# Half of the second feed-forward product by seven block products, their sums made by GpSimd, and four inverse levels with VectorE's transpose

## The chip, the core and the metric

One core of a Trainium2 chip runs the whole kernel. The metric is the device time of one execution in microseconds, the median of the runs shown. Five engines work beside each other, each on its own list of instructions: TensorE (PE; its weight loads are shown apart as PEld), VectorE (DVE), ScalarE (ACT), GpSimd (POOL) and SyncE (SP), which here only issues transfers.

## The reference

All arithmetic is in float32. One decoder block on 256 tokens of width 2048: a gated DeltaNet branch and a sliding-window attention branch, merged by gates, then a feed-forward part with squared ReLU. What the change touches is the last product, and the triangular solve of the DeltaNet branch.

```python
# _gdn_chunked
sol = lax.linalg.triangular_solve(eye + a_kk, rhs, left_side=True, lower=True, unit_diagonal=True)
...
# reference
h = _rmsnorm(x, ln2_w[l])
u = jax.nn.relu(jnp.einsum("bsd,df->bsf", h, w_ff1[l]))      # w_ff1 (2048, 8192)
x = x + jnp.einsum("bsf,fd->bsd", jnp.square(u), w_ff2[l])   # w_ff2 (8192, 2048)
```

## The kernel before, in words

**The stream of weights.** Every weight matrix comes from memory in tiles of four 128-row blocks by 512 columns (1 MB), into four buffers `raw` that are filled in turn. SP issues the transfers in program order; each waits on `lo_ready` until the tile that lies in its buffer is split. A tile is worked in two pieces of [128, 2 blocks, 512]. Float32 precision is kept by splitting each piece in a high and a low part: ScalarE copies the piece to `hi` (line 745, rounded), VectorE takes the difference `lo = raw - hi` (line 1126). Both have four buffers (`PIECES`), so ScalarE and VectorE stay up to four pieces ahead of TensorE: ScalarE waits on `piece_used`, VectorE on `hi_ready`, TensorE on `lo_ready`. Each engine's list is written out by hand: the function `ahead` puts the split of piece m + 4 and whatever step belongs at place m one behind the other, so that a step which waits holds up all splits behind it.

**A product.** `group` (line 387 is its matmul) takes a 512-column output for both token tiles t = 0, 1 into the two banks `acc[:, t]`. One piece against one token tile is six matmuls of 128x128 weights and 512 columns (two blocks, times high-high, low-high and high-low).

**The feed-forward part** runs in two halves of 4096 hidden columns. In each half eight groups (8 pieces each) make `us = relu(...)`, 512 columns at a time; VectorE squares them to `uq` (line 1648); after the first pair of pieces of the next group, TensorE turns `uq` by eight 128x128 transposes (line 403) into the two banks `tb`, from which ScalarE and VectorE write `u_hi` and `u_lo`. Then four groups (`GG0`, `GG1`) of 16 pieces multiply these by `w_ff2`, 512 output columns each, and VectorE adds both banks to `x1`.

**The inverse.** In the stage from about 440 to 665 us the triangular inverse of each head pair is built in `LEVELS` = 6 levels, for four head pairs. A level has `level_a` (line 624, behind GpSimd's masked product `Ls`, line 366) and `level_b`, whose lines 633 and 636 form the correction and its transpose; VectorE subtracts both from the two copies `both_[:, 1]` and `both_[:, 0]`. These steps lie between the matmuls of other groups. GpSimd has nothing to do behind this stage.

## Time and profile before

| what | value |
| --- | --- |
| median of 3 runs | 1557.05 us (1555.12 to 1557.07) |
| the profiled execution, whole | 1553.01 us |
| its span in the trace | 1551.3 us |
| TensorE busy | 1531.9 us, 99% |
| VectorE busy | 927.0 us, 60% |
| ScalarE busy | 741.5 us, 48% |
| GpSimd busy | 55.9 us, 4% |

The span is the part of the profiled execution that the trace covers, from its first to its last instruction or transfer. The profiled execution is one of its own and 4 us below the median, so a sum made on the trace is carried over to the median as a difference. Matmuls overlap their neighbours: a matmul's duration (0.39 us) is longer than the distance from one start to the next, and it is the distance that counts.

### The profile page before, as it was taken

Reading aid. Unit: us, or ns where it says so; the run is one execution under the profiler, and the core shown is the slowest. Engines: PE = TensorE matmul, PEld = TensorE weight load, DVE = VectorE, ACT = ScalarE, POOL = GpSimd, SP = SyncE. Lnnn points to the kernel's source line nnn. Section 1 sums busy time; section 2 is a strip of 40 time slices with the busy share of each in tenths; the row PEclk is TensorE's granted clock in tenths of the full one; section 3 lists DMA queues with packets and bytes.
Section 4 is the critical chain, followed back from the end, with each engine's and each line's share of the span. In section 5 each row is a group of like instructions: output and inputs, shape, how many; then the busy total and the mean of one; then the engine's idle time right before and its main releaser. Section 6 shows DMA issues by size and latency. Waiting matters only on the chain.

```text
span 1551.3 us, 19383 instructions
## 1 busy us (share of the span) xinstructions
PE 1531.9 (99%) x7244; PEld 1277.6 (82%) x7244; DVE 927.0 (60%) x1110; ACT 741.5 (48%) x827; POOL 55.9 (4%) x97
## 2 busy tenths in 40 slices
PE   7999999999999999999999999999999999999999
PEld 5888888888888888878888888888888888888887
DVE  5866645777786876866555555544444555554443
ACT  5554444667654444453445444443333444443332
POOL 5000000000040110100000000000000000000000
PEclk9999999999999999999999999999999999999999
DMA  7565554444544444444655655555556556556552
GB/s 255 190 206 183 189 182 163 156 156 150 164 162 136 147 143 143 136 162 163 244 186 167 198 181 189 189 190 190 189 190 193 186 190 189 187 183 212 204 199 72
DMA packets 140521, 275.96 MB, mean 178 GB/s; under 512 B 7088, under 2 KB 7600, under 8 KB 140208
## 3 DMA queue, kind: packets, MB, share of 16 engines
q1 hardware_dynamic: 136160, 272.71, 52.9%
q10 hardware_dynamic: 4304, 2.47, 0.5%
q8 instruction: 38, 0.62, 0.2%
q14 instruction: 19, 0.16, 0.0%
HBM read 273.06 MB, written 2.10 MB: 177 GB/s over the span
## 4 chain that ended last, share of the span: by engine, by line
PE 96%; DVE 2%; DMA 1%; ACT 1%; ACTq 0%; issue 0%; SPq 0%; DVEq 0%
PE acc L387 88%; PE wk L403 2%; DMA raw<-in_w_in 1%; PE wk L636 1%; PE wk L633 1%; PE wk L624 1%; DVE lo L1126 1%; PE wk L508 1%; PE wk L481 1%; PE wk L468 0%; DVE st_lo L1164 0%; ACT hi L745 0%; PE wk L492 0%; PE wk L519 0%; PE wk L615 0%; PE wk L643 0%
## 5 line engine op out<-in xcount | busy, mean ns | idle before, releaser
L1126 DVE TENSOR_TENSOR lo<-raw,hi 128x1024 fp32r<-128x1024 f32 x512 | 624.8, 1224 | 549.7 <-ACT hi L745 532.0
L745 ACT ACTIVATE hi<-raw 128x1024 fp32r<-128x1024 f32 x512 | 541.9, 1060 | 647.7 <-PE acc L387 645.6
L387 PE MATMUL acc<-hi,st_hi 128*128 128x512 f32 x1312 | 524.5, 400 | 5.6 <-DVE lo L1126 2.9
L387 PE MATMUL acc<-lo,st_hi 128*128 128x512 f32 x1312 | 511.6, 390 | 0.0
L387 PE MATMUL acc<-hi,st_lo 128*128 128x512 f32 x1312 | 511.1, 390 | 0.0
L387 PEld LDWEIGHTS acc<-hi,st_hi 128*128 128x128 f32 x1312 | 246.7, 188 | 55.7 <-DVE lo L1126 4.4
L387 PEld LDWEIGHTS acc<-lo,st_hi 128*128 128x128 f32 x1312 | 246.2, 188 | 52.2
L387 PEld LDWEIGHTS acc<-hi,st_lo 128*128 128x128 f32 x1312 | 246.8, 188 | 47.9 <-issue 1.0
L387 PE MATMUL acc<-hi,u_hi 128*128 128x512 f32 x512 | 199.3, 389 | 0.0
L387 PE MATMUL acc<-lo,u_hi 128*128 128x512 f32 x512 | 199.2, 389 | 0.0
L387 PE MATMUL acc<-hi,u_lo 128*128 128x512 f32 x512 | 199.2, 389 | 0.0
L387 PEld LDWEIGHTS acc<-lo,u_hi 128*128 128x128 f32 x512 | 96.1, 188 | 20.1
L387 PEld LDWEIGHTS acc<-hi,u_hi 128*128 128x128 f32 x512 | 96.1, 188 | 19.9
L387 PEld LDWEIGHTS acc<-hi,u_lo 128*128 128x128 f32 x512 | 96.1, 188 | 19.8
L387 PE MATMUL acc<-hi,mix_hi 128*128 128x512 f32 x128 | 50.2, 392 | 0.0
L387 PE MATMUL acc<-lo,mix_hi 128*128 128x512 f32 x128 | 49.9, 390 | 0.0
L387 PE MATMUL acc<-hi,mix_lo 128*128 128x512 f32 x128 | 49.8, 389 | 0.0
L366 POOL TENSOR_TENSOR Ls<-pair,lmask 128x256 f32<-128x256 f32 x24 | 22.2, 932 | 184.7 <-DVE pair L1468 122.2
L387 PE MATMUL acc<-hi,oa_hi 128*128 128x512 f32 x64 | 25.3, 395 | 3.4 <-DVE oa_lo L1141 3.4
L1141 DVE TENSOR_TENSOR both__109<-both__109,wk 128x256 f32<-128x256 f32 x48 | 19.9, 416 | 14.4 <-PE wk L633 14.2
L387 PEld LDWEIGHTS acc<-lo,mix_hi 128*128 128x128 f32 x128 | 24.0, 188 | 5.0
L387 PEld LDWEIGHTS acc<-hi,mix_lo 128*128 128x128 f32 x128 | 24.0, 188 | 4.9
(246 smaller groups left out, 1048.7 us busy)
## 6 DMA issues: line engine op xcount, KB each, us to landing
raw<-in_w_ff SPq DMA_DIRECT2D x128, 1024.0 KB, 5.1
raw<-in_w_in SPq DMA_DIRECT2D x100, 1024.0 KB, 5.0
raw<-in_w_out SPq DMA_DIRECT2D x16, 1024.0 KB, 5.0
raw<-in_w_gdn_proj SPq DMA_DIRECT2D x8, 1024.0 KB, 5.0
raw<-in_w_swa_proj SPq DMA_DIRECT2D x4, 1024.0 KB, 5.0
x_tok<-in_x SPq DMA_DIRECT2D x2, 1024.0 KB, 7.1
x<-in_x SPq DMA_DIRECT2D x1, 2048.0 KB, 7.9
out_x<-x ACTq DMA_DIRECT2D x3, 512.0 KB, 3.6
```

Source lines behind the costliest of these rows:

```text
L366: pool.tensor_tensor(Ls[:, l % 2], pair[:], bcast(lmask[:, l, :], 1, [P, 2, P]), ALU.mult).then_inc(ev["n_Ls"], 1)
L387: last = pe.matmul(acc[:, t], w[:, k0 + 2 * m + kk, P * t:P * t + P], v[:, i % PIECES, kk, :], start=m == 0 and kk == 0 and a == 0, stop=m ...
L403: last = pe.transpose(dst[:, b, P * t:P * t + P], src(t, b), ident[:])
L481: last = pe.matmul(wk[:, 2 + g * nk // N, g * nk % N:g * nk % N + nk], qc[:, g, P * t:P * t + P], swa_qk[:, 1, HS * g + h, 0:nk], start=Tr ...
L508: last = pe.matmul(wk[:, 4, 0:P], pt[:, P * b:P * b + P], swa_v[:, kt, at:at + P], start=b == 0, stop=b == NG * (t + 1) - 1)
L624: last = pe.matmul(blk(W[0], h), Ls[:, l % 2, h, :], diag[:, 1, h, :], start=True, stop=True)
L633: last = pe.matmul(blk(W[3], h), diag[:, 0, h, :], Pc[:, h, :], start=True, stop=True)
L636: last = pe.matmul(blk(W[2], h), Pc[:, h, :], diag[:, 0, h, :], start=True, stop=True)
L745: act.activation(hi[:, i % PIECES], raw[:, i // 2 % RAW, 2 * (i % 2):2 * (i % 2) + 2, :], ACT.Copy)\
L1126: dve.tensor_tensor(lo[:, i % PIECES], raw[:, i // 2 % RAW, 2 * (i % 2):2 * (i % 2) + 2, :], hi[:, i % PIECES].bitcast(F32), ALU.subtract) ...
L1141: dve.tensor_tensor(out_, a, b, op).then_inc(done, 1)
```

## The change

**The second product** is now made from tiles of `w_ff2` for two neighbouring 512-column groups at a time. The 4096 rows of a half are cut into eight octets of four 128-row blocks. For the even octets the product [2 token tiles x 2 pairs of row blocks] by [2 pairs of row blocks x 2 column groups] is formed by seven block products in place of eight, in the variant of Winograd; the odd octets are multiplied as before. Each of the seven products has one piece of weights and one token tile's weights load: six matmuls. Four of the seven weight pieces (t1, t2, t4, t3) are sums of parts of the octet's two tiles; GpSimd makes them (`weight_sums`, 128x1024 elements each, in four buffers `t_sums`), one behind the other, and they are then split by ScalarE and VectorE like a loaded piece. The matching sums of the squared activations are made by GpSimd too (`token_sums`, 128x256 each), from a copy that ScalarE writes; ScalarE and VectorE split them. The products end in eight banks (p1 to p7, c22), so `acc` and `wk` are both full during this stage. After the last even octet of a column pair VectorE (`first_sums`, `second_sums`) and GpSimd (`shared_sums`) combine the banks into `x1`. A half now has 88 pieces where it had 64, and 720 large matmuls where it had 768. The tiles of an even octet are loaded when the octet two before it has been split and (`octet_used`) its sums are made. The squares are written over `us`, `uq` is gone, and the transposes of the last group come after the second piece of the second product.

**The inverse:** in the levels 0 to 3 the transposed correction (line 636, two matmuls, and the VectorE subtraction of it) is left out, and VectorE transposes `both_[:, 1]` into `both_[:, 0]` instead. This is exact there since everything lies within 32x32 blocks.

```diff
+IN_BLOCKS = 4
+
+OCTETS = 8
+PAIR_PIECES = 11
+HALF_PIECES = 2 * OCTETS // 2 * PAIR_PIECES
+MORE_PIECES = HALF_PIECES - 64
+PRODUCTS = ("b11", "b21", "b22", "t1", "t2", "t4", "t3")
...
+        def pieces_of(half):
+            return [(np_, o, n) for np_ in range(2) for o in range(OCTETS) for n in range(4 if o % 2 else 7)]
...
+        def source(half, np_, o, n):
+
+            t = tile0(half, np_, o)
+            if o % 2 == 0 and n >= 3:
+                return t_sums[n - 3][:], ev["t_made"], sums_before(half, np_, o) + n - 2
+            which, k = (n // 2, 2 * (n % 2)) if o % 2 else ((0, 0), (0, 2), (1, 2))[n]
+            return raw[:, (t + which) % RAW, k:k + 2, :], landed[(t + which) % RAW], 16 * ((t + which) // RAW) + 16
...
+            def octet_used(half, np_, o, which):
+
+                a = piece0(half) + octet0(np_, o)
+                if o % 2:
+                    sp.wait_ge(lo_ready, a + 2 * which + 2)
+                else:
+                    sp.wait_ge(lo_ready, a + 2 + which)
+                    sp.wait_ge(ev["t_made"], sums_before(half, np_, o) + 3 + which)
 
...
+            def token_sums(half, k):
+
+                n = 4 * half + k
...
+                    pool.wait_ge(lo_ready, piece0(0) + octet0(1, 6) + 5)
+                pool.tensor_tensor(s1, a21, a22, ALU.add).then_inc(ev["s_made"], 1)
+                pool.tensor_tensor(s3, a11, a21, ALU.subtract).then_inc(ev["s_made"], 1)
+                pool.wait_ge(ev["s_made"], 4 * n + 1)
+                pool.tensor_tensor(s2, s1, a11, ALU.subtract).then_inc(ev["s_made"], 1)
+                pool.wait_ge(ev["s_made"], 4 * n + 3)
+                pool.tensor_tensor(s4, a12, s2, ALU.subtract).then_inc(ev["s_made"], 1)
...
+            def weight_sums(half, np_, o):
+
+                t = tile0(half, np_, o)
+                made = sums_before(half, np_, o)
+                b11, b21 = raw[:, t % RAW, 0:2, :], raw[:, t % RAW, 2:4, :]
+                b12, b22 = raw[:, (t + 1) % RAW, 0:2, :], raw[:, (t + 1) % RAW, 2:4, :]
+                t1, t2, t4, t3 = (t[:] for t in t_sums)
+
...
+                def free(n):
+                    if np_ or o:
+                        pool.wait_ge(lo_ready, piece0(half) + octet0(*divmod(OCTETS * np_ + o - 2, OCTETS)) + 4 + n)
+                    elif n == 0:
...
+                pool.wait_ge(landed[t % RAW], 16 * (t // RAW) + 16)
+                pool.wait_ge(landed[(t + 1) % RAW], 16 * ((t + 1) // RAW) + 16)
+                free(0)
+                pool.tensor_tensor(t1, b12, b11, ALU.subtract).then_inc(ev["t_made"], 1)
+                free(1)
+                pool.wait_ge(ev["t_made"], made + 1)
+                pool.tensor_tensor(t2, b22, t1, ALU.subtract).then_inc(ev["t_made"], 1)
+                free(2)
+                pool.wait_ge(ev["t_made"], made + 2)
+                pool.tensor_tensor(t4, b21, t2, ALU.subtract).then_inc(ev["t_made"], 1)
+                free(3)
+                pool.tensor_tensor(t3, b22, b12, ALU.subtract).then_inc(ev["t_made"], 1)
+
+            def shared_sums(half, np_):
+                n = 2 * half + np_
+                pool.wait_ge(ev["c_first"], 5 * n + 4)
+                x12, x21, x22 = x1_part(np_, 0, 1), x1_part(np_, 1, 0), x1_part(np_, 1, 1)
+                pool.tensor_tensor(x12, x12, sum2[:], ALU.add).then_inc(ev["c_pooled"], 1)
+                pool.wait_ge(ev["c_first"], 5 * n + 5)
+                pool.tensor_tensor(x21, x21, sum3[:], ALU.add).then_inc(ev["c_pooled"], 1)
+                pool.tensor_tensor(x22, x22, sum3[:], ALU.add).then_inc(ev["c_pooled"], 1)
+
+            for half in range(2):
...
+                        if l < IN_BLOCKS:
+                            return
...
+            def products(half, np_, o, gf):
+
...
+                for m, name in enumerate(PRODUCTS):
+                    if o == 0:
...
+                            pe.wait_ge(ev["c_first"], 5 * n)
+                        if name == "b21":
+                            if np_:
+                                pe.wait_ge(ev["c_second"], 4 * n - 3)
+                            else:
+                                pe.wait_ge(acc_free, 2 * (gf + 8) + 1)
+                        if name == "b22":
+                            if np_:
+                                pe.wait_ge(ev["c_second"], 4 * n - 1)
+                            else:
+                                pe.wait_ge(acc_free, 2 * (gf + 8) + 2)
+                        if name == "t4" and np_ == 0:
+                            pe.wait_ge(ev["u_lo"], 8 * half + 8)
+                    pe.wait_ge(lo_ready, a0 + m + 1)
+                    slot = (a0 + m) % PIECES
+                    wh, wl = factor(u_hi, None, o, combos[name]), factor(u_lo, u_lo6, o, combos[name])
+                    alone = name in ("b11", "t1", "t2", "t3")
+                    for kk in range(2):
+                        for a, (w, v) in enumerate(((wh, hi), (wl, hi), (wh, lo))):
+                            last = pe.matmul(banks[name], w[:, kk, :], v[:, slot, kk, :],
+                                             start=o == 0 and kk == 0 and a == 0,
+                                             stop=alone and o == OCTETS - 2 and kk == 1 and a == 2)
...
+                    pe.wait_ge(ev["u_lo"], 8 * half + o + 1)
+                for j, banks in enumerate(((p2, p4), (p3, c22))):
+                    for t in range(TT):
+                        for m in range(2):
+                            if t == 0:
+                                pe.wait_ge(lo_ready, a0 + 2 * j + m + 1)
+                            begins = o == 1 and j == 1 and t == 1
+                            if begins and m == 0 and n:
+                                pe.wait_ge(ev["c_second"], 4 * n)
+                            slot = (a0 + 2 * j + m) % PIECES
+                            for kk in range(2):
...
+                def parts():
+                    n = 4 * half + g // 2
+                    act.wait_ge(ev["u_turned"], g + 8 * half + 1)
+                    if g:
+                        act.wait_ge(ev["s_made"], 4 * n)
+                    elif half:
+                        act.wait_ge(lo_ready, piece0(0) + octet0(1, 6) + 4)
+                    act.activation(u_copy[:], tbv, ACT.Copy).then_inc(ev["uc_made"], 1)
+                    act.activation(u_hi[g][:, 0:2], tbv[:, :, 0:P].rearrange("p (c k) t -> p c k t", c=2), ACT.Copy)
+                    act.activation(u_hi[g][:, 2], tbv[:, 2:4, P:2 * P], ACT.Copy).then_inc(ev["u_hi"], 1)
+                return plain if g % 2 else parts
...
+            def piece(half, p):
+                src, sem_, value = source(half, *pieces_of(half)[p])
+                act.wait_ge(sem_, value)
+                act.wait_ge(piece_used, piece0(half) + p + 1)
+                act.activation(hi[:, (piece0(half) + p) % PIECES], src, ACT.Copy).then_inc(hi_ready, 1)
...
-                        less(1, ev["n_S2"], ev["n_Ma"])
+                        less(1, (ev["n_S2"], 6 * i + l + 1), ev["n_Ma"])
                         if l < LEVELS - 1:
                             diagonal(1, l + 1, ev["n_Ra"], (ev["n_Ma"], 6 * i + l + 1))
-                        less(0, ev["n_S3"], ev["n_Mb"])
+                        if l < IN_BLOCKS:
+                            dve.wait_ge(ev["n_Ma"], 6 * i + l + 1)
+                            dve.transpose(flat(both_[:, 0]), flat(both_[:, 1])).then_inc(ev["n_Mb"], 1)
+                        else:
+                            less(0, (ev["n_S3"], (LEVELS - IN_BLOCKS) * i + l - IN_BLOCKS + 1), ev["n_Mb"])
...
+            def u_square(g, n):
                 dve.wait_ge(acc_free, 2 * g + 4)
...
+            def piece(half, p):
+                src, _, _ = source(half, *pieces_of(half)[p])
+                a = piece0(half) + p
+                dve.wait_ge(hi_ready, a + 1)
+                dve.tensor_tensor(lo[:, a % PIECES], src, hi[:, a % PIECES].bitcast(F32), ALU.subtract)\
+                    .then_inc(lo_ready, 1)
...
+                def of_p5():
+                    dve.wait_ge(piece_used, a + 4)
+                    dve.tensor_tensor(x12, p5, x12, ALU.add).then_inc(ev["c_first"], 1)
+                    dve.tensor_tensor(x22, p5, x22, ALU.add).then_inc(ev["c_first"], 1)
+
+                def of_p1_p6():
+                    dve.wait_ge(ev["c_copied"], n + 1)
+                    dve.tensor_tensor(x11, p1, x11, ALU.add).then_inc(ev["c_first"], 1)
+                    dve.wait_ge(piece_used, a + 5)
+                    dve.tensor_tensor(sum2[:], p6, sum2[:], ALU.add).then_inc(ev["c_first"], 1)
+
+                def of_p7():
+                    dve.wait_ge(ev["c_first"], 5 * n + 4)
+                    if n:
+                        dve.wait_ge(ev["c_pooled"], 3 * n)
+                    dve.wait_ge(piece_used, a + 7)
+                    dve.tensor_tensor(sum3[:], p7, sum2[:], ALU.add).then_inc(ev["c_first"], 1)
+                return of_p5, of_p1_p6, of_p7
...
+            def second_sums(half, np_):
+
+                n = 2 * half + np_
+                a = piece0(half) + octet0(np_, OCTETS - 1) + PIECES
+
+                def add(t, j, bank, sem_, value, pooled):
+                    def step():
+                        part = x1_part(np_, t, j)
+                        dve.wait_ge(sem_, value)
+                        if pooled:
+                            dve.wait_ge(ev["c_pooled"], 3 * n + pooled)
+                        else:
+                            dve.wait_ge(ev["c_first"], 5 * n + 3)
+                        dve.tensor_tensor(part, bank, part, ALU.add).then_inc(ev["c_second"], 1)
+                    return step
+                return (add(0, 0, p2, ev["c_done"], 2 * n + 1, 0), add(1, 0, p4, piece_used, a + 2, 2),
+                        add(0, 1, p3, ev["c_done"], 2 * n + 2, 1), add(1, 1, c22, piece_used, a + 4, 3))
+
...
+                for np_ in range(2):
+                    at = octet0(np_, OCTETS - 1)
+                    of_p5, of_p1_p6, of_p7 = first_sums(half, np_)
+                    c11, c21, c12, c22_ = second_sums(half, np_)
+                    steps |= {at: of_p5, at + 1: of_p1_p6, at + 2: of_p7, at + 3: c11}
```

Where a column pair of the second product ends and the next begins, VectorE's list was, at the end of one group of 16 pieces (`lo` is a split; x1 the result):

```order
L1126 TENSOR_TENSOR lo_51<-raw_49,hi_50 128x1024 [waits hi_ready] x12
L1626 TENSOR_TENSOR x1_128<-acc,x1_128 128x512 [waits acc0_done,x_back]
L1126 TENSOR_TENSOR lo_51<-raw_49,hi_50 128x1024 [waits hi_ready]
L1630 TENSOR_TENSOR x1_128<-acc,x1_128 128x512 [waits piece_used]
L1126 TENSOR_TENSOR lo_51<-raw_49,hi_50 128x1024 [waits hi_ready]
```

It is now, at the same place (`t_sums0` to `t_sums3` are GpSimd's sums t1, t2, t4, t3 of the next column pair's first octet):

```order
L1922 TENSOR_TENSOR lo_51<-raw_49,hi_50 128x1024 [waits hi_ready]
L1963 TENSOR_TENSOR x1_128<-acc,x1_128 128x512 [waits c_first,c_done]
L1922 TENSOR_TENSOR lo_51<-t_sums0_154,hi_50 128x1024 [waits hi_ready]
L1963 TENSOR_TENSOR x1_128<-wk,x1_128 128x512 [waits c_pooled,piece_used]
L1922 TENSOR_TENSOR lo_51<-t_sums1_155,hi_50 128x1024 [waits hi_ready]
L1963 TENSOR_TENSOR x1_128<-acc,x1_128 128x512 [waits c_pooled,c_done]
L1922 TENSOR_TENSOR lo_51<-t_sums2_156,hi_50 128x1024 [waits hi_ready]
L1963 TENSOR_TENSOR x1_128<-wk,x1_128 128x512 [waits c_pooled,piece_used]
```

The add of `acc` on the sixth row, for which TensorE's third product of the next column pair waits (`c_second`), has moved behind the splits of t1 and t2.

GpSimd's list had nothing at this place; it now has this, from the last even octet of a column pair over the end to the first octet of the next:

```order
L483 TENSOR_TENSOR t_sums_154<-raw 128x1024 [waits lo_ready,landed1,landed0]
L486 TENSOR_TENSOR t_sums_155<-raw,t_sums_154 128x1024 [waits t_made,lo_ready]
L489 TENSOR_TENSOR t_sums_156<-raw,t_sums_155 128x1024 [waits t_made,lo_ready]
L491 TENSOR_TENSOR t_sums_157<-raw 128x1024 [waits lo_ready]
L497 TENSOR_TENSOR x_128<-x_128,sum_131 128x512 [waits c_first]
L499 TENSOR_TENSOR x_128<-x_128,sum_132 128x512 [waits c_first]
L500 TENSOR_TENSOR x_128<-x_128,sum_132 128x512
L483 TENSOR_TENSOR t_sums_154<-raw 128x1024 [waits lo_ready,landed1,landed0]
```

The three adds onto x stand between the four weight sums of one column pair and those of the next.

At the start of the second product TensorE's list had the transposes of the last squares behind 24 matmuls, of which the last three stand here:

```order
L387 MATMUL acc<-hi,u_hi 128x512
L387 MATMUL acc<-hi,u_lo 128x512
L387 MATMUL acc<-lo,u_hi 128x512
L403 MATMUL wk<-ident,uq 128x128 [waits u_lo,u_squared]
L403 MATMUL wk<-ident,uq 128x128 x7
L387 MATMUL acc<-hi,u_hi 128x512 [waits lo_ready]
```

Now they come behind 12 matmuls (the first, and the last three, stand here):

```order
L904 MATMUL wk<-hi,u_hi_133 128x512 [waits lo_ready,s_lo,u_lo]
L904 MATMUL acc<-hi,u_hi_133 128x512
L904 MATMUL acc<-hi,u_lo_141 128x512
L904 MATMUL acc<-lo,u_hi_133 128x512
L546 MATMUL wk<-ident,us 128x128 [waits u_lo,u_squared]
L546 MATMUL wk<-ident,us 128x128 x7
L904 MATMUL acc<-hi,u_hi_133 128x512 [waits lo_ready,acc_free]
```

VectorE's list at that place is now this; the square of `us` for which the transposes wait stands behind the split of `t_sums0`:

```order
L1909 TENSOR_TENSOR u_lo6_s4_151<-u_sums_153,u_hi6_139 128x256
L1922 TENSOR_TENSOR lo_51<-raw_49,hi_50 128x1024 [waits hi_ready]
L1922 TENSOR_TENSOR lo_51<-t_sums0_154,hi_50 128x1024 [waits hi_ready]
L1916 TENSOR_TENSOR us_130<-us_130 128x1024 [waits acc_free]
L1922 TENSOR_TENSOR lo_51<-t_sums1_155,hi_50 128x1024 [waits hi_ready]
L1922 TENSOR_TENSOR lo_51<-t_sums2_156,hi_50 128x1024 [waits hi_ready]
L1391 TENSOR_TENSOR u_lo7_148<-wk,u_hi7_140 128x1024 [waits u_hi]
L1922 TENSOR_TENSOR lo_51<-t_sums3_157,hi_50 128x1024 [waits hi_ready]
```

The square has the place that it had, behind the split of the fourth piece, but that piece and the two behind the square are now sums of GpSimd.

## Rows read from the trace of the kernel before

**Rows 1.** The page: span, busy time by engine, and the chain that ended last.
```profile
span 1551.3 us, 19383 instructions
...
PE 1531.9 (99%) x7244; PEld 1277.6 (82%) x7244; DVE 927.0 (60%) x1110; ACT 741.5 (48%) x827; POOL 55.9 (4%) x97
...
PE 96%; DVE 2%; DMA 1%; ACT 1%; ACTq 0%; issue 0%; SPq 0%; DVEq 0%
```

**Rows 2.** Windows, second product: length, PE, PEld, DVE, ACT, POOL, clock, DMA share, GB/s.
```profile
1017.00:1188.00 171.00, 171.00 (x760) 141.66 (x760) 83.07 (x71) 68.58 (x66) 0.00 (x0) 1.00 0.58 194
```

**Rows 3.** The timeline in the second half's second product: start us, length us.
```profile
1479.70 0.39 PE L387 MATMUL acc<-hi,u_hi 128*128 128x512 f32 x1
...
1481.26 1.06 ACT L745 ACTIVATE hi<-raw 128x1024 fp32r<-128x1024 f32 x1 [3.02 <-PE acc L387]
...
1482.35 2.59 DVE L1126 TENSOR_TENSOR lo<-raw,hi 128x1024 fp32r<-128x1024 f32 x2 [2.85 <-ACT hi L745]
...
1485.60 0.39 PE L387 MATMUL acc<-lo,u_hi 128*128 128x512 f32 x1
```

**Rows 4.** The page's groups of instructions: count, busy us, mean ns, idle before.
```profile
L1126 DVE TENSOR_TENSOR lo<-raw,hi 128x1024 fp32r<-128x1024 f32 x512 | 624.8, 1224 | 549.7 <-ACT hi L745 532.0
L745 ACT ACTIVATE hi<-raw 128x1024 fp32r<-128x1024 f32 x512 | 541.9, 1060 | 647.7 <-PE acc L387 645.6
```

**Rows 5.** The timeline of TensorE at one inverse level.
```profile
457.47 0.60 PE L633 MATMUL wk<-Pc,diag 128*128 128x128 f32 x4
457.91 0.61 PE L636 MATMUL wk<-diag,Pc 128*128 128x128 f32 x4
458.28 0.48 PE L387 MATMUL acc<-hi,st_hi 128*128 128x512 f32 x1
```

**Rows 6.** The timeline of VectorE and GpSimd where both work, first level.
```profile
452.56 0.42 DVE L1141 TENSOR_TENSOR diag<-pair,lbase 128x256 f32<-128x256 f32 x1
452.61 1.86 POOL L366 TENSOR_TENSOR Ls<-pair,lmask 128x256 f32<-128x256 f32 x2 [8.30 <-DVE pair L1468]
...
453.01 0.45 DVE L1473 STREAM_TRANSPOSE both__109<-diag 128x256 f32<-128x256 f32 x1
...
453.38 0.48 DVE L1141 TENSOR_TENSOR both__109<-ident,diag 128x256 f32<-128x256 f32 x1
...
453.79 0.96 DVE L1141 TENSOR_TENSOR both__109<-ident,both__109 128x256 f32<-128x256 f32 x1
```

**Rows 7.** The same, where GpSimd comes behind one of the splits.
```profile
521.43 1.22 DVE L1126 TENSOR_TENSOR lo<-raw,hi 128x1024 fp32r<-128x1024 f32 x1
...
521.85 1.40 POOL L366 TENSOR_TENSOR Ls<-pair,lmask 128x256 f32<-128x256 f32 x1 [4.44 <-PE wk L624]
...
522.57 0.68 DVE L1539 TENSOR_REDUCE small<-o_sq 128x4 f32<-128x512 f32 x1
```

**Rows 8.** GpSimd's instructions by shape: busy us, mean ns.
```profile
L325 POOL MEMSET rmask<- 128x768 f32 x1 | 0.7, 739 | 0.0
...
L326 POOL MEMSET below<- 128x128 f32 x1 | 0.2, 207 | 0.0
```

**Rows 9.** One tile's instructions (Ls): duration ns min/median/max.
```profile
L366 POOL TENSOR_TENSOR Ls<-pair,lmask x24: 727/923/1403, 452.6 to 650.5; 128x256 f32<-128x256 f32 x24
```

**Rows 10.** The timeline where the second product begins, at 1017.3 us.
```profile
1019.16 1.22 DVE L1126 TENSOR_TENSOR lo<-raw,hi 128x1024 fp32r<-128x1024 f32 x1 [0.71 <-ACT hi L745]
...
1020.30 1.22 DVE L1648 TENSOR_TENSOR uq<-us 128x1024 f32<-128x1024 f32 x1
...
1022.74 1.03 PE L403 MATMUL wk<-ident,uq 128*128 128x128 f32 x8
```

**Rows 11.** The page's DMA issues: KB each, us from issue to landing.
```profile
raw<-in_w_ff SPq DMA_DIRECT2D x128, 1024.0 KB, 5.1
```

**Rows 12.** VectorE's adds onto x1 in the same stretch: count, busy us, mean ns.
```profile
L1626 DVE TENSOR_TENSOR x<-acc,x 128x512 f32 (+1 forms) x3 | 2.1, 691 | 1.4 <-PE acc L387 1.4
```

**Rows 13.** The waits: engine, line, what it waited for: us in total, times, longest.
```profile
PE wk L409 <- DMA rows<-in_conv_w: 3.7, 1, 3.7
```

305 lines of the change are left out of this document (216 added, 89 removed).

## The prediction

> **What bounds the kernel now.** I read the page first: TensorE is busy 99% of the span and makes 96% of the chain that ended last [rows 1]. The windows view of one second product shows the same locally: TensorE busy for all of 171 us at granted clock 1.00 (its full level, 2.4 GHz), VectorE 83 us, ScalarE 69 us, GpSimd nothing [rows 2]. The timeline gives the pace: 27 large matmuls start between 1479.70 and 1485.60 us, so one costs 0.227 us and six, the work of one piece against one token tile, 1.36 us. The splits stand idle between pairs: a copy of 1.06 us starts behind the matmuls that free its buffer, the two VectorE splits follow it [rows 3, 4]. So fewer matmuls shorten the kernel as long as the pieces keep coming. That is the question.
>
> **What TensorE saves.** Before, each half of the second product has 768 large matmuls, now 720. 96 fewer by 0.227 are 21.8 us. The transposed correction goes in four levels of four head pairs: 16 times, each from 457.91 to the next large matmul at 458.28, 0.37 us [rows 5]: 5.9 us. Its replacement on VectorE is a transpose of 0.45 us for a subtraction that costs as much as its neighbours of 0.42 [rows 6], with one wait fewer; TensorE does not wait there for VectorE, so this part costs nothing, and if its cover were gone 16 times 0.03 us. Together TensorE has 27.7 us less to do.
>
> **What GpSimd has to do.** Sixteen times (2 halves, 2 column pairs, 4 even octets) it makes four sums of 128x1024. No row has that shape. The shortest product of 128x256 took 0.73 us [rows 9]. Without a fixed part the new sum costs four times that, 2.9 us: the upper bound. The two memsets give a fixed part of 0.10 us (0.207 for 128 elements, 0.739 for 768) [rows 8], which makes 2.6 us. Below, GpSimd took 0.73 us where VectorE takes 0.42 [rows 6, 9], and 1.7 times VectorE's 1.22 us [rows 4] is 2.1 us. I take 2.4 us, between 2.1 and 2.6 and much nearer to these than to 2.9. The Trainium skill (GPSIMD Engine Reference, Elementwise — side-by-side cycle accounting) measured 4497 ns for a tensor_tensor of 2048 elements; by it and the row of 0.73 us a sum of 1024 would be an estimated 2.3 us. No run here shows that shape.
>
> **Whether VectorE and GpSimd can work at once.** Here I choose, and most of the forecast hangs on it. At 521.43 us VectorE begins a split, which reads two SBUF tensors, and would be done at 522.57, where its next instruction starts. GpSimd begins its product at 521.85 and takes 1.40 us instead of 0.73: it ends at 523.25, which is 0.73 us after 522.52 [rows 7, 9]. It waited for the split. The other way round, two products of GpSimd take 1.86 us from 452.61 to 454.47; VectorE's subtraction from 453.79 takes 0.96 us where such an instruction takes 0.42, and ends 0.28 us after GpSimd [rows 6]. So the two take turns, also between back-to-back instructions, and a split holds its turn some 1.1 us (521.43 to 522.52). The Trainium skill states this as a rule (SBUF — State Buffer, Who interferes with whom): a VectorE instruction with two SBUF inputs contends with a GpSimd instruction that reads SBUF, and whoever is first keeps the port for its whole length. The trace agrees, with 0.67 us lost by GpSimd and 0.54 by VectorE; by the rule no turn is shared, without it the case below called "beside each other" holds.
>
> **The pair of octets.** An even octet with its odd neighbour has 42 + 48 matmuls: 20.4 us of TensorE. In it stand 11 splits and 4 sums: 11 x 1.1 + 4 x 2.4 = 21.7 us of turns. That is 1.3 us too much even if no turn is left unused. Some is: GpSimd starts only when both tiles have landed, 5.1 us behind the issue [rows 11], which waits for the last sum of the octet two before; in that gap the splits stop once four pieces are ahead. Then come four sums and four splits alternately, 14 us, of which three pieces in stock cover only part. Following the waits forward through the lists with these durations I get between 0 and 4 us per pair, 25.6 us for the sixteen, 1.6 each.
>
> **The start of a half's second product (T).** TensorE now reaches the transposes of the last squares 12 matmuls behind T, at T + 2.7, before at 5.4. The square ended 4.2 us behind the start (1020.30 + 1.22 less 1017.3) [rows 10], so 1.5 us are lost in any case. With turns more: t2 can only begin when the activations' sums are split, about T - 1.0 (`s_lo`). It ends at T + 1.4, split of b22 to 2.5, t4 to 4.9, split of t1 to 6.0, t3 to 8.4, and only then the square, 9.6. Wait: 6.9 us, twice, 13.8 us.
>
> **The end of a column pair (E).** The third product of the next pair waits for the add of `acc`, and that stands on VectorE behind the splits of t1 and t2, whose sums stand on GpSimd behind the three shared adds. Those adds end at about E + 3.0 (128x512 each, 1.3 us by the same scaling, between splits). t1 to E + 5.4, t2 to 7.9, split of t1 to 9.0, t4 to 11.4, split of t2 to 12.5, the add of 0.69 us [rows 12] to 13.2. TensorE has two products of 1.36 us, then waits 10.5 us. This happens once in each half: 21 us. Between the halves the next pieces are loaded ones, so the wait ends with the shared adds and one add: 2.7 us. SP's queue is not late by this: tiles of odd octets wait only for splits.
>
> **The sum.** 25.6 + 13.8 + 21 + 2.7 = 63.1 us of new waits against 27.7 us saved: +35.4 us. The profiled execution took 1553.0 us (span 1551.3 and 1.7 around it), which becomes 1588.4; carried over to the median of 1557.05 it is **1592 us**. The tail is as before, one add and one small store behind the last matmul. The longest wait of TensorE in the trace is 3.7 us [rows 13], shorter than the new ones; the clock stayed at its full level. The Trainium skill (TensorE: Matmul & The Clock Gate, Why this matters for your kernels) warns that an idle TensorE falls back to the lower clock, 1.2 GHz; no row here shows it or prices it, and it isn't in the sum.
>
> **The rivals.**
> 1. *Beside each other:* GpSimd's larger sums don't hold up the splits. Then 9.6 us of sums fit in 20.4 and the pairs cost nothing; the start costs 1.5 us twice, the column pair 6.4 twice (shared adds to E + 1.4, t1 and t2 to 6.2, copy, split and add 2.9), the halves 1.6: 17.4 against 27.7, -10.3 us, **1547 us**, faster. It is decided at the first sum that meets a split: lengthened or not; the time turns faster once the new waits stay under 27.7 us. For it speaks only that no row has two large instructions meeting; against it rows 6 and 7. Chance 0.18.
> 2. *Turns, but short ones:* with 2.1 us a pair needs 12.1 + 8.4 = 20.5 us of turns, and costs little. Start 6.0 and column pair 9.3, twice each, and halves 2.5 make 33.1: +5 if the pairs cost nothing and +18 if they cost 0.8 each: 1562 to 1575 us, say **1569**. The lower bound of the sum speaks for it; the row of 0.73 us, of which at most 0.1 is fixed by the memsets, against. Chance 0.13.
> 3. *Long turns:* 2.9 us per sum. A pair needs 23.7 us, 3.3 more than TensorE, 53 us for sixteen; by the same chains the start grows to 8.4, the column pair to 12.3, the halves to 2.9: 97 less 27.7, +69.4, **1626 us**. For it speaks that no fixed part of this instruction is shown by itself, against it the memsets. Chance 0.09.
>
> My forecast has 0.60; its own range, with sums of 2.25 to 2.65 us and turns of 1.0 to 1.2, is +20 to +56: 1577 to 1613 us. The range **1551 to 1613** holds it, the second rival and a part of the first, should its waits come out longer: 0.60 + 0.13 + 0.06. Within 0.2% (3 us, about what can be told from no change) lies only a mixture of the first two, 0.04. Faster 0.17, slower 0.79.
>
> **What would show it.** In the profile after: GpSimd's sums of 128x1024 at 2.3 to 2.6 us alone and about 3.5 where a split is in front; splits of 1.22 us lengthened to over 3 in bursts of four; TensorE idle some 7 us before the transposes of `us` and some 10 us before the third product of the second column pair, behind line 1963; 1440 large matmuls at 0.227 us. Wrong would be: splits all at 1.22 us, or TensorE waiting for tiles.

## The result, and the profile after

| what | before | after |
| --- | --- | --- |
| median | 1556.66 us (4 runs, 1555.12 to 1557.07) | 1601.06 us (4 runs, 1600.74 to 1603.71) |
| ratio, 95% interval | | 1.0293 [1.0278, 1.0309] |
| profiled execution | 1553.0 us | 1600.8 us |
| its span | 1551.3 us | 1599.0 us |
| mean granted clock | 1.000 | 0.987 |

The kernel became 44.4 us slower. The forecast was 1592 us, in the range 1551 to 1613. The profiled span grew by 47.7 us, and the accounts below are made on it. A ratio is estimated from all runs and can differ by about 0.001 from the quotient of the two medians.

The page of the changed kernel: span, busy time by engine, the chain that ended last, and the two groups of splits (count, busy us, mean ns, idle before).

```profile
span 1599.0 us, 18799 instructions
...
PE 1524.8 (95%) x7084; PEld 1260.0 (79%) x7084; DVE 1124.0 (70%) x1198; ACT 805.6 (50%) x903; POOL 294.0 (18%) x205
...
PE 80%; DVE 14%; ACT 2%; issue 2%; POOL 1%; DMA 1%; ACTq 0%; SPq 0%; DVEq 0%
...
L1922 DVE TENSOR_TENSOR lo<-raw,hi 128x1024 fp32r<-128x1024 f32 x112 | 233.5, 2119 | 29.8 <-ACT hi L1322 25.6
...
L1922 DVE TENSOR_TENSOR lo<-t_sums,hi 128x1024 fp32r<-128x1024 f32 x64 | 91.7, 1453 | 15.4 <-ACT hi L1322 11.9
```

Against [rows 1], TensorE has 160 matmuls fewer and is busy 7 us less, but the span is 48 us longer: it is idle for 74 us where it was idle for 19. Its part of the chain that ended last fell from 96% to 80%, and VectorE's rose from 2% to 14%. The splits of the loaded pieces in the second product, the same instruction on the same shape as in [rows 4], went from 1224 ns to a mean of 2119 ns.

GpSimd's sums, one row for each of the four: duration in ns (least, median, most), first and last start.

```profile
L483 POOL TENSOR_TENSOR t_sums<-raw x16: 2367/2424/3454, 1005.4 to 1562.9; 128x1024 f32<-128x1024 f32 x16
L486 POOL TENSOR_TENSOR t_sums<-raw,t_sums x16: 2344/3190/3210, 1016.1 to 1566.5; 128x1024 f32<-128x1024 f32 x16
L489 POOL TENSOR_TENSOR t_sums<-raw,t_sums x16: 3144/3192/3215, 1018.6 to 1569.8; 128x1024 f32<-128x1024 f32 x16
L491 POOL TENSOR_TENSOR t_sums<-raw x16: 3315/3378/3394, 1021.8 to 1573.0; 128x1024 f32<-128x1024 f32 x16
```

The first sum usually runs by itself and takes 2.4 us, which is what the prediction took. Behind it the splits catch up, and a sum takes 3.2 to 3.4 us.

TensorE's waits: us in total, times, longest.

```profile
PE acc L904 <- DVE x L1963: 18.8, 4, 8.7
PE acc L928 <- DVE lo L1922: 16.3, 16, 1.6
PE wk L546 <- DVE us L1916: 12.5, 2, 6.3
...
PE acc L904 <- DVE lo L1922: 4.3, 5, 0.9
```

Each row is one of the predicted waits: the end of the column pair (line 1963), the pairs of octets (lines 928 and 904 for a split) and the start of a half's second product (line 546). No row says that TensorE waits for a tile.

The timeline where the second product begins, T = 1017.10 us: start, length, and in brackets the idle time before.

```profile
1016.12 2.41 POOL L486 TENSOR_TENSOR t_sums<-raw,t_sums 128x1024 f32<-128x1024 f32 x1 [8.28 <-DVE u_lo_s L1909]
...
1017.09 2.52 DVE L1922 TENSOR_TENSOR lo<-raw,hi 128x1024 fp32r<-128x1024 f32 x1 [1.05 <-ACT hi L1322]
...
1018.61 3.21 POOL L489 TENSOR_TENSOR t_sums<-raw,t_sums 128x1024 f32<-128x1024 f32 x1
...
1019.53 3.37 DVE L1922 TENSOR_TENSOR lo<-t_sums,hi 128x1024 fp32r<-128x1024 f32 x1
1019.59 0.39 PE L904 MATMUL acc<-lo,u_hi 128*128 128x512 f32 x1
1021.78 3.31 POOL L491 TENSOR_TENSOR t_sums<-raw 128x1024 f32<-128x1024 f32 x1
...
1022.83 3.35 DVE L1916 TENSOR_TENSOR us<-us 128x1024 f32<-128x1024 f32 x1
...
1026.24 1.97 PE L546 MATMUL wk<-ident,us 128*128 128x128 f32 x8 [6.26 <-DVE us L1916]
```

Sums and VectorE's instructions overlap in the records, but each ends about one length of its own behind the end of the other: the t2 sum ends at 1018.53, and the split that starts at 1017.09 ends at 1019.61, 1.08 us later; t4 ends at 1021.82, 2.2 us behind that; the next split at 1022.90; t3 at 1025.09; the square at 1026.18. TensorE's last matmul before the transposes starts at 1019.59, and the transposes at 1026.24.

The timeline at the end of the first column pair, E = 1117.4 us.

```profile
1120.12 2.38 POOL L483 TENSOR_TENSOR t_sums<-raw 128x1024 f32<-128x1024 f32 x1
...
1120.95 0.40 PE L904 MATMUL acc<-lo,u_hi 128*128 128x512 f32 x1
...
1122.64 2.34 POOL L486 TENSOR_TENSOR t_sums<-raw,t_sums 128x1024 f32<-128x1024 f32 x1
...
1125.99 0.68 DVE L1963 TENSOR_TENSOR x<-wk,x 128x512 f32<-128x512 f32 x1
...
1129.27 0.68 DVE L1963 TENSOR_TENSOR x<-acc,x 128x512 f32<-128x512 f32 x1
...
1130.01 0.79 PE L904 MATMUL acc<-hi,u_hi 128*128 128x512 f32 x1 [8.66 <-DVE x L1963]
...
1130.60 0.63 PE L904 MATMUL acc<-hi,u_lo 128*128 128x512 f32 x1
...
1135.29 0.43 PE L904 MATMUL wk<-hi,u_hi 128*128 128x512 f32 x1
```

The t1 sum ends at E + 5.1 us, t2 at E + 7.6, the add onto `x` at E + 12.5, and TensorE goes on at E + 12.6. (Of the four waits for line 1963, two are these of 8.7 us; the other two, 0.74 us each, come one product earlier, for the first add.) The last two rows show something else: behind this wait the matmuls start 0.43 us apart, not 0.227, for the first twelve. The windows view of this place gives the reason (length, TensorE's busy time and instructions, granted clock, DMA share, GB/s).

```profile
1125.00:1130.00 5.00, 0.00 (x0) 0.51 0.08 10
1130.00:1135.00 5.00, 4.99 (x12) 0.50 0.97 329
1135.00:1140.00 5.00, 5.00 (x23) 0.96 0.21 81
```

TensorE has been idle since 1121.3 us. The granted clock is still 1.00 in the window from 1120 to 1125 us, 0.51 in the next, and 0.50 in the first 5 us behind the wait. 0.50 is the lower level, 1.2 GHz.

### The profile page after: what moved, and what is told of

Read it like the earlier page. It is cut to its first block, busy times and chain, and to the rows that moved or that the text cites. A ratio compares the mean times of both kernels' runs of the same rounds, so it can differ in the third digit from the quotient of the medians.

```text
span 1599.0 us, 18799 instructions
## 1 busy us (share of the span) xinstructions
PE 1524.8 (95%) x7084; PEld 1260.0 (79%) x7084; DVE 1124.0 (70%) x1198; ACT 805.6 (50%) x903; POOL 294.0 (18%) x205
## 4 chain that ended last, share of the span: by engine, by line
PE 80%; DVE 14%; ACT 2%; issue 2%; POOL 1%; DMA 1%; ACTq 0%; SPq 0%; DVEq 0%
PE acc L530 62%; DVE lo L1922 9%; PE wk L904 4%; PE acc L904 3%; PE wk L928 2%; PE acc L928 2%; PE wk L546 2%; DVE lo L1374 1%; ACT hi L1322 1%; DMA raw<-in_w_in 1%; PE wk L776 1%; PE wk L651 1%; DVE diag L1391 0%; PE wk L624 0%; PE wk L767 0%
## 5 line engine op out<-in xcount | busy, mean ns | idle before, releaser
L1374 DVE TENSOR_TENSOR lo<-raw,hi 128x1024 fp32r<-128x1024 f32 x384 | 473.2, 1238 | 360.1 <-ACT hi L955 351.4
L955 ACT ACTIVATE hi<-raw 128x1024 fp32r<-128x1024 f32 x384 | 405.9, 1058 | 439.6 <-PE acc L530 431.4
L1922 DVE TENSOR_TENSOR lo<-raw,hi 128x1024 fp32r<-128x1024 f32 x112 | 233.5, 2119 | 29.8 <-ACT hi L1322 25.6
L1322 ACT ACTIVATE hi<-raw 128x1024 fp32r<-128x1024 f32 x112 | 118.9, 1061 | 136.6 <-PE wk L928 108.5
L1922 DVE TENSOR_TENSOR lo<-t_sums,hi 128x1024 fp32r<-128x1024 f32 x64 | 91.7, 1453 | 15.4 <-ACT hi L1322 11.9
L1322 ACT ACTIVATE hi<-t_sums 128x1024 fp32r<-128x1024 f32 x64 | 67.7, 1060 | 51.6 <-PE acc L904 22.6
L928 PE MATMUL acc<-hi,u_hi 128*128 128x512 f32 x128 | 51.5, 403 | 16.3 <-DVE lo L1922 16.3
L483 POOL TENSOR_TENSOR t_sums<-raw 128x1024 f32<-128x1024 f32 x16 | 43.0, 2687 | 114.9 <-DMA raw<-in_w_ff 90.3
L904 PE MATMUL wk<-hi,u_hi 128*128 128x512 f32 x160 | 62.9, 393 | 0.0
L904 PE MATMUL wk<-lo,u_hi 128*128 128x512 f32 x160 | 62.8, 392 | 0.0
L491 POOL TENSOR_TENSOR t_sums<-raw 128x1024 f32<-128x1024 f32 x16 | 53.9, 3370 | 0.0
L904 PE MATMUL wk<-hi,u_lo 128*128 128x512 f32 x136 | 53.4, 393 | 0.0
L489 POOL TENSOR_TENSOR t_sums<-raw,t_sums 128x1024 f32<-128x1024 f32 x16 | 51.0, 3187 | 2.2
```

The costliest lines, as they stand in the source:

```text
L483: pool.tensor_tensor(t1, b12, b11, ALU.subtract).then_inc(ev["t_made"], 1)
L489: pool.tensor_tensor(t4, b21, t2, ALU.subtract).then_inc(ev["t_made"], 1)
L491: pool.tensor_tensor(t3, b22, b12, ALU.subtract).then_inc(ev["t_made"], 1)
L904: last = pe.matmul(banks[name], w[:, kk, :], v[:, slot, kk, :], start=o == 0 and kk == 0 and a == 0, stop=alone and o == OCTETS - 2 and kk ...
L928: last = pe.matmul(banks[t], w[:, 2 * m + kk, P * t:P * t + P], v[:, slot, kk, :], start=begins and m == 0 and kk == 0 and a == 0, stop=o ...
L955: act.activation(hi[:, i % PIECES], raw[:, i // 2 % RAW, 2 * (i % 2):2 * (i % 2) + 2, :], ACT.Copy)\
```

## The experiments

Each ratio is against runs of the kernel before on the same chip.

| run | what it does | us | ratio, 95% interval |
| --- | --- | --- | --- |
| e7 | before, with GpSimd reading beside it | 1591.31 | 1.0231 [1.0210, 1.0251] |
| e8 | before, with GpSimd writing beside it | 1555.52 | 1.0001 [0.9991, 1.0012] |
| e2 | the change, sums of a few elements | 1562.03 | 1.0041 [1.0027, 1.0055] |
| e4 | the change, sums replaced by writes as long | 1558.31 | 1.0022 [1.0013, 1.0032] |
| e3 | the change, sums of half the size | 1569.65 | 1.0095 [1.0079, 1.0110] |
| e1 | the inverse part alone | 1551.78 | 0.9977 [0.9968, 0.9986] |
| e5 | the change, square ahead | 1592.78 | 1.0245 [1.0229, 1.0260] |
| e6 | the change, adds ahead | 1596.16 | 1.0251 [1.0228, 1.0275] |
| e9 | the change, both ahead | 1588.94 | 1.0226 [1.0210, 1.0242] |
| e10 | before, one long wait in each half | 1577.84 | 1.0144 [1.0128, 1.0159] |
| e11 | before, short waits in each half | 1566.25 | 1.0073 [1.0059, 1.0087] |

The theory: GpSimd's sums and VectorE's two-input instructions on SBUF take turns, so the splits come late. The main rival: the new order and the new dependences (a sum must be finished before it is split) are what costs, whatever the engines share.

### Does a reading GpSimd hold up the splits by itself? (e7, e8)

The kernel before, in its own order, with 60 instructions on GpSimd during the first half's second product, on buffers of their own, for which nobody waits.

```diff
+            pool.wait_ge(lo_ready, 8 * QG0)
+            for n in range(60):
...
+                pool.tensor_tensor(pads[2][:], pads[0][:], pads[1][:], ALU.subtract)      # e7
...
+                for m in range(3):                                                       # e8
+                    pool.memset(pads[2][:, 0:2 - m // 2], 1.0)
```

> The kernel before, with 60 idle-time sums of 128x1024 on GpSimd that read two SBUF tensors nobody else uses, one behind the other, from the start of the first second product on. Nothing waits for them. Theory of turns: a sum (2.4 us) and a split (1.1 us) take turns, so a pair of splits takes 7.0 us where TensorE needs 5.44; 60 sums meet 60 splits, 30 pairs lose 1.56 us each, some 45 us: about 1602 us, splits in that stretch show about 3.5 us. Rival (the waits of the changed kernel come only from waiting for GpSimd's results, in order): nobody waits here, so 1557 us and splits of 1.22 us.

> As the reading stream, but each of the 60 sums is replaced by memsets of 2560 elements per partition in all, which take as long (about 2.4 us by the rows of before) and read nothing. Theory of turns, in the form that only reading instructions take them: 1557 us, splits stay 1.22 us. Rival (any GpSimd instruction holds VectorE up): about 1602 us.

e7 took 1591.31 us against 1554.94 (only 2 runs, 1589.40 and 1593.21), e8 1555.52. So 60 sums cost 36.4 us, 0.61 us each, with no dependence on them and no order changed; the same number of writes, 2.4 us each time, cost nothing that can be measured. The expectation of 45 us for e7 was too high: one turn of each takes 3.3 to 3.4 us and not 3.5, and pieces in stock cover part of it. In the profiled execution (1593.21 us) the new waits, by the starts of the matmuls, are about 27 us; about 8 us more are a lower clock behind the four longest waits, of 2.9 and 3.5 us (behind the last, at 1183.34 us, thirteen matmuls start 0.43 us apart). The timeline of e7:

```profile
1024.86 19.89 POOL L375 TENSOR_TENSOR pad<-pad,pad 128x1024 f32<-128x1024 f32 x6
...
1025.78 3.37 DVE L1656 TENSOR_TENSOR uq<-us 128x1024 f32<-128x1024 f32 x1
...
1029.08 6.72 DVE L1134 TENSOR_TENSOR lo<-raw,hi 128x1024 fp32r<-128x1024 f32 x2
...
1035.71 1.21 DVE L1149 TENSOR_TENSOR u_lo<-wk,u_hi 128x1024 fp32r<-128x1024 f32 x1
```

Six sums take 3.3 us each, VectorE's square 3.37 us, two splits 3.36 us each. The fourth row is VectorE's subtraction of `u_hi` from the transposed values, which lie in a PSUM bank: GpSimd reads all the while, and it takes 1.21 us, as ever. The page of e8 has the splits at their old length:

```profile
L1137 DVE TENSOR_TENSOR lo<-raw,hi 128x1024 fp32r<-128x1024 f32 x512 | 625.0, 1224 | 552.4 <-ACT hi L756 534.7
```

This is the first link of the prediction ("the two take turns"), shown by itself: it is reading that they share, and the rival can't make e7.

### How much of the change is that? (e2, e4, e3)

In e2 each sum is made over 2 x 4 elements of a partition instead of 1024 (but for the first octet of each half, so in 14 of 16 places and not 15); in e3 over half of it (1 x 512), with the same exception; in e4 each is two and a half memsets of the same 2.4 us in all. The rest of the sum tiles is left as it was, so the weights that TensorE uses are not the right ones; all instructions, waits and transfers else are those of the change.

```diff
-                pool.tensor_tensor(t1, b12, b11, ALU.subtract)
+                pool.tensor_tensor(t1[:, a, b], b12[:, a, b], b11[:, a, b], ALU.subtract)   # e2, e3
...
+                pool.memset(t1, 1.0)                                                        # e4
+                pool.memset(t1, 1.0)
+                pool.memset(t1[:, 0:1, :], 1.0)
```

> The changed kernel with GpSimd's four weight sums cut to 8 elements per partition in 15 of the 16 columns-and-octet places of each kind (all but the first octet of each half), so the products are not the reference's. Theory of turns: only the first octet's wait (2 x 6.4 us), a shorter wait at the end of a column pair and small ones remain, 27 us of TensorE's waits where 62 us were: 1601 - 35 and some 3 us less lost to the clock, about 1563 us; splits back to 1.22 us. Rival (splits are slow for another reason, the loads or ScalarE): splits of 3 us remain and about 1590 us.

> The changed kernel with each weight sum replaced by memsets that take about as long (2.5 us) and read nothing, so the products are not the reference's; order and waits as they are. Theory of turns: the pairs cost nothing, the start 1.5 us twice, the column pair about 7 us twice, 20 us of waits in place of 62 and less lost to the clock: 1555 to 1560 us. Rival (the in-order chains and GpSimd's pace are the cause, not the shared reading): still about 1600 us.

> The changed kernel with the weight sums of all but the first octet of each half cut to half their elements (128x512, 1.3 us), so the products are not the reference's. Theory of turns held for the whole length: a pair of octets needs 12.0 + 5.2 = 17.2 us of turns, below TensorE's 20.4, so the pairs' waits vanish and the column pair's shrinks: 33 us of TensorE's waits where 62 were, about 1570 us. Rival (what costs is each handing over, not its length): the number of turns is the same, so about 1590 us or more.

e4 keeps the order, the dependences and the length of GpSimd's work and takes only the weight sums' reading away (the small sums of the activations and the adds onto `x` still read): 1558.31 us, ratio 1.0022. Of the 44 us, 41 go. TensorE's waits in it:

```profile
PE acc L920 <- DVE x L1979: 15.4, 4, 7.0
...
PE wk L562 <- DVE us L1932: 2.8, 2, 1.4
```

The waits of the pairs are gone altogether, the start's fell from 6.3 to 1.4 us, and the end of the column pair keeps 7.0 of 8.7 us: there the sums stand one behind the other on GpSimd, and 2.4 us each is enough to be late. e2 turns this round. Its sums are short but its first octet keeps whole ones, so the start still waits 6.3 us, while the column pair waits 3.7 us and the pairs not at all: 1562.03 us. The splits of its sums are back at a median of 1225 ns. e3 stands between: 1569.65. Its sums, by themselves 1.3 us and behind a split 2.1 to 2.3 us:

```profile
L484 POOL TENSOR_TENSOR t_sums<-raw x16: 1287/1307/2407, 1004.1 to 1529.0; 128x512 f32<-128x512 f32 x14, 128x1024 f32<-128x1024 f32 x2
...
L492 POOL TENSOR_TENSOR t_sums<-raw x16: 2246/2269/3323, 1020.4 to 1534.7; 128x512 f32<-128x512 f32 x14, 128x1024 f32<-128x1024 f32 x2
```

The first lies mostly alone, the last behind a split. With half the size a pair needs 11 x 1.1 + 4 x 1.3 = 17.3 us of turns against 20.4 us of TensorE, and the pairs' waits are gone but for 1.2 us. That is the balance from the prediction: it is the sum of the two engines' reading that must fit under TensorE's time, not each engine's own. And even e4, whose weight sums share nothing, is 3.4 us slower than before: what is saved, 21.8 us and the inverse, is lost again in waits (21.5 us by the starts of the matmuls, most of it at the ends of the column pairs) and in the clock. e4 is also what the rival "beside each other" describes. That rival's sum gave 10.3 us faster; it had 17.4 us for these waits, 5.9 for the inverse and nothing for the clock, which costs about 6 us behind e4's waits of 7.0 us (twice) and of 2.1 us between the halves.

### The inverse part (e1)

```diff
+                        if l < IN_BLOCKS:
+                            return
...
+                            dve.transpose(flat(both_[:, 0]), flat(both_[:, 1])).then_inc(ev["n_Mb"], 1)
```

> The kernel before with the inverse part of the change alone. My theory: TensorE has 16 pairs of small matmuls less, 0.37 us each, and waits for nobody: 5.9 us faster, 1551 us where before gives 1556.7; the trace of the changed kernel shows the DeltaNet stage ending only about 4 us earlier, so 4 to 6 us. Rival: VectorE's chain holds the level back and TensorE waits there for what it saves: no change.

1551.78 us (11 runs) against 1555.43 (15 runs): -3.7 us, the only version here that beats both kernels. It comes short of the 5.9 us of TensorE's work that it removes, since the stage has new small waits. In its waits view:

```profile
PE acc L388 <- DVE gates L1422: 1.6, 4, 0.8
PE wk L625 <- DVE diag L1144: 0.5, 1, 0.5
```

The waits for `gates` are 0.8 us more than in the kernel before (there 0.8 us, once), and a wait of 0.5 us for `diag` is new; the rest of the shortfall was not looked for. VectorE's list in this stage was not as far ahead as the prediction thought.

### Can another order save the change? (e5, e6, e9)

e5 puts the last square ahead of the split of t1. e6 puts all three adds behind one split at the end of a column pair, ahead of the splits of the sums. e9 does both.

```diff
+                    if then is not None and m == n - 1:                                # e5
+                        early()
...
-                    steps |= {at: of_p5, at + 1: of_p1_p6, at + 2: of_p7, at + 3: c11}
-                    steps |= {at + 4: c21, at + 5: c12, at + 6: c22_}
+                    steps |= {at: of_p5, at + 1: of_p1_p6, at + 2: of_p7}              # e6
+                    steps |= {at + 3: lambda a=(c11, c21, c12): [step() for step in a], at + 4: c22_}
```

> The changed kernel with the square of the last activations placed ahead of the split of t1 in VectorE's list. My theory (the square is held up by the splits and sums in front of it): the wait at each start falls from 6.4 to some 3 us, 7 us less in all and a shorter stretch at the lower clock: 1591 to 1594 us. Rival (t1, t2 and the others then come late by as much, the wait only moves): 1599 to 1601 us.

> The changed kernel with the adds of the second and third bank placed ahead of the splits of t1 and t2. My theory: the wait of 8.8 us for the add is gone, but the sums t1 to t3 stand on GpSimd behind the shared adds all the same and arrive one turn after the other, so the wait moves to the next four products, in shorter pieces that keep the clock up: 1595 to 1599 us. Rival (the add's place alone costs the time): the 17.6 us and the clock come back, about 1580 us.

> The changed kernel with both moves in VectorE's list: the square ahead of the split of t1, and the adds ahead of the splits of t1 and t2. My theory: the two act at different places and add up, 8 and 5 us: about 1588 us, still some 32 us above the kernel before, since the pairs' waits (about 25 us) and the turns stay. Rival (with the long waits gone the kernel comes near the one before): 1570 us or less.

Each against before on its own chip, e5 is 37.4 us slower, e6 40.7 (its runs lie from 1589.51 to 1598.33 us) and both together 33.9, where the change was 44.4: 7.0, 3.7 and 10.5 us are won back. The waits of e9:

```profile
PE wk L904 <- DVE lo L1924: 13.3, 8, 3.4
PE acc L928 <- DVE lo L1924: 12.7, 12, 1.6
...
PE wk L546 <- DVE us L1918: 6.0, 2, 3.0
```

The start's wait fell from 6.3 to 3.0 us. The long wait for the add is gone, but TensorE reaches the split of t1 sooner and waits for that instead, 3.4 us at most, and the splits behind it are late too: 13.3 us in a new row. The order decides where TensorE waits; the turns decide how long. No order tried comes within 30 us of the kernel before.

### The clock (e10, e11)

The kernel before, where in each second product TensorE waits for a chain of memsets on GpSimd: one wait of about 9 us (e10), or four of about 2 us (e11). Nothing else is changed.

```diff
+                for j, length in ((2, 12),):                          # e10; e11: ((2, 5), (3, 5), (4, 5), (5, 5))
+                    pool.wait_ge(lo_ready, 8 * qg + 2 * j + 4)
+                    for _ in range(length):
...
+                        pool.memset(pad[:], 1.0).then_inc(ev["padded"], 1)
...
-                group(qg, gg_, 16, u_hi, u_lo, after={1: u_turn(half, 7), 13: wait_u})
+                group(qg, gg_, 16, u_hi, u_lo, after={1: u_turn(half, 7), 13: wait_u} |
+                      {2 * j + 1: lambda n=n: pe.wait_ge(ev["padded"], 12 * half + n) for j, n in {2: 12}.items()})
```

> The kernel before, with one wait of TensorE put in each second product, about 9 us long, on a chain of 12 memsets of GpSimd that read nothing. Theory (a long wait costs its length and then a stretch at the lower clock, as the changed kernel's trace shows at 1130 us): 18 us for the waits and about 2.5 us each for matmuls at 0.43 us, some 23 us: 1579 us, and granted clock near 0.5 in the wait. Rival (the clock's fall in the changed kernel has another reason): 18 us, 1574 us, clock 1.00.

> The kernel before, with the same wait in four pieces in each second product, one per pair of pieces, each about 2.2 us. Theory: the clock stays at its full level through each, and only the 18 us of waiting are lost: 1574 us, some 5 us below the long waits. Rival (what counts is the sum of idle time, not the length of one): the same time and clock as with the long waits.

e10 took 22.8 us more than before, for waits of 18.3 us (twice 9.1). The 4.5 us that are left are the clock's. Windows around its first wait, and the timeline behind it:

```profile
1035.00:1040.00 5.00, 2.88 (x13) 1.00 0.63 210
1040.00:1045.00 5.00, 0.00 (x0) 0.76 0.59 209
1045.00:1050.00 5.00, 2.97 (x7) 0.50 0.00 0
1050.00:1055.00 5.00, 5.00 (x17) 0.72 0.00 0
```

```profile
1047.03 0.79 PE L398 MATMUL acc<-hi,u_hi 128*128 128x512 f32 x1 [9.14 <-POOL pad L377]
1047.62 0.63 PE L398 MATMUL acc<-hi,u_lo 128*128 128x512 f32 x1
```

The clock stays at 1.00 up to 1040 us and is at 0.50 when TensorE comes back; thirteen matmuls take the 5.7 us from 1047.03 to 1052.74 instead of 2.9. That is 2.8 us. The second wait of the same trace is as long, 9.14 us, but behind it, from 1414.60 us, only seven more matmuls start slowly and the clock costs 1.7 us. Together these are the 4.5 us: waits of one length cost different amounts.

In e11 only two of the four waits in a half were real: the other chains had started early enough to be over when TensorE came (the second ran from 1038.83 to 1043.83 us, and TensorE would have needed it at 1043.9). So it has 8.3 us of waits in place of 18, and its expectation of 1574 us failed for that reason; it took 1566.25 us, 11.2 more than before. Its timeline behind the first wait, of 2.09 us:

```profile
1038.44 0.50 PE L398 MATMUL acc<-hi,u_hi 128*128 128x512 f32 x1 [2.09 <-POOL pad L377]
1038.78 0.39 PE L398 MATMUL acc<-hi,u_lo 128*128 128x512 f32 x1
```

The second matmul behind the wait starts 0.34 us after the first and the third 0.23 us after that, with the clock at 1.00 in all windows from 1035 to 1055 us. The third of its four waits, at the same place of the second half and also of 2.09 us, was followed by a lower clock all the same:

```profile
1395.00:1400.00 5.00, 2.91 (x12) 0.93 0.56 203
1400.00:1405.00 5.00, 5.00 (x18) 0.73 0.67 210
```

Seven matmuls start 0.43 us apart there, which costs 1.6 us. So both long waits of e10 cost more than their length, and of the four short ones of e11 one did. The expectation that a short wait leaves the clock up held in three cases of four.

## Why the prediction was right, and what it left out

The direction and the mechanism held; 1601 lies 9 us above the likeliest value, inside its own range of 1577 to 1613 us. For each term, "measured" is the distance between two starts of matmuls less 0.227 us, added over the gaps. Part of the nearness is luck: the waits came out 4.7 us shorter than forecast, while the clock, which the sum left out, cost about 8.

| term | predicted | measured |
| --- | --- | --- |
| 96 large matmuls fewer | -21.8 | not apart (their pitch is 0.227 where the clock is 1.00) |
| the inverse | -5.9 | -4.2 in the stage, -3.7 alone (e1) |
| waits of the pairs | +25.6 | +23.9 |
| start of a half's second product | +13.8 | +12.8 |
| end of the column pair | +21.0 | +19.4 |
| between the halves | +2.7 | +2.3 |
| slower clock behind the four long waits | none | +7.8 |
| first matmul behind each shorter wait | none | +2.4 |
| slower clock elsewhere | none | about +4 in this trace |

- *Turns.* Taken from two meetings of small instructions [rows 6, 7]; e7 shows it between large ones, e8 shows that it takes reading, e4 that it carries 41 of the 44 us. The rule of the Trainium skill (SBUF — State Buffer, Who interferes with whom) that the two contend agrees with the traces: the split went from 1.22 to 3.4 us beside a sum. The rival "beside each other" is out: its point of decision was whether a sum that meets a split is lengthened, and it is, from 2.4 to 3.2 us and more. For "turns, but short ones" and "long turns" the row of 2.4 us decides.
- *The size of a sum.* 2.4 us was taken between 2.1 and 2.6, and 2.4 was measured (0.73 us for a quarter, 1.3 for half of it).
- *The chains.* At the start the square was to end at T + 9.6 and ended at T + 9.1; at the column pair the add was to end at E + 13.2 and ended at E + 12.5. Both times the splits held a turn for 1.08 us and a sum behind one for 2.2, where 1.1 and 2.4 were used: the four terms of the waits are 7 to 17% too high in the sum.
- *The clock.* "The clock stayed at its full level", and its fall "isn't in the sum": this is the step that failed. It was named, with the rule of the Trainium skill (TensorE: Matmul & The Clock Gate, Why this matters for your kernels) that warns of it, but not priced, since no row before had it. Behind each of the four waits of 6 and 9 us TensorE starts at the lower clock: behind the two of 8.7 us for twelve matmuls and for six, behind the two of 6.3 us for the eight transposes and then three and five matmuls. That makes 7.8 us. Another 2.4 us come from the shorter waits, at a clock of 1.00: the second matmul behind one starts 0.31 to 0.34 us after the first and not 0.227.
- *The clock elsewhere.* It also fell at 30 to 40 us and at 690 to 710 us, about 1 and 3 us, and this isn't the change's doing. The profiled execution of the kernel before has neither fall and is quicker than its median (1553.0 against 1556.66 us); the trace of e8, whose time is that of the kernel before, has both, with windows of 0.83 from 30 to 40 and from 700 to 710 us. These falls probably make up most of the 3.3 us by which the span grew more than the median.
- *The inverse.* "TensorE does not wait there for VectorE, so this part costs nothing": mis-sized, 4.2 us for 5.9. The waits of the kernel before had already one for VectorE in this stage (`gates`, 0.8 us, once); now TensorE waits there 1.3 us more.

The account of the span: the second product begins at 1017.10 us, 0.2 us sooner than before (the inverse gave 4.2, the clock and the start took 4). From there 58.4 of waits, 7.8 of clock and 2.4 behind the shorter waits, less 21.8, make 46.8, so 46.6 in all, of 47.7 us. The last 1.1 us was not looked for.

Not tried: the sums on an engine other than GpSimd, sums whose inputs come from PSUM, and a version in which only as many octets are made by seven products as fit under TensorE's time. By e4's number, which is slower than before with no turns to take at all in the pairs, the last probably has little to gain; that is argued and not shown.

## What to carry to other kernels

Before work is moved to an idle engine, add up the time for which it and its neighbour hold what they share: here GpSimd was 96% idle and VectorE 40%, yet 12.1 us of splits and 9.6 us of sums did not fit under 20.4 us of TensorE. An algorithm that saves a multiplication and costs sums pays here 9.6 us of GpSimd for 1.36 us of TensorE per octet, so it needs the sums to be free, and even then (e4) the first and last of a chain must have cover. Price each new wait of the bound engine with what the clock does behind it, and time the parts of a change alone: the small part here was a gain (e1).

## What the runs showed of the hardware that was not expected

- Among the instructions of VectorE that met a reading GpSimd in e7 and in the changed kernel's second product, only those with both inputs in SBUF were lengthened: with one in PSUM the subtraction took 1.21 us (e7) and the add onto `x` 0.68 us in the middle of a sum of 3.14 us (at 1125.99). The square, both of whose inputs are `us`, took 3.37 us.
- The same wait of 3.4 us of TensorE, for `oa_lo` at about 692 us, was followed by a lower clock in the changed kernel and not in e1. The windows of the one and of the other:

```profile
690.00:700.00 10.00, 6.62 (x21) 0.75 0.43 142
700.00:710.00 10.00, 10.00 (x41) 0.91 0.38 130
```

```profile
690.00:700.00 10.00, 6.62 (x30) 1.00 0.42 128
700.00:710.00 10.00, 10.00 (x46) 1.00 0.51 188
```

  Of the 13 traces with this wait, 3.4 us in each, eight show the lower clock behind it (among them e8, whose second product is at its old pace) and five, the kernel before among them, do not. What decides it stays open. Of e11's four waits of 2.1 us one was followed by a lower clock; the 18 waits of 5.4 to 9.1 us in the second products of all traces always were.
- Memsets of GpSimd cost VectorE nothing (splits 1224 ns with and without); this one e8 had expected.
